# Prompt attention of a hybrid decoder step: values weighed on column halves of the array, sums of probabilities on GpSimd

## The reference, cut to what matters

```python
def fox_prompt(q, k, v, logf):          # q, k, v: (1, 2048, 8, 64)
    ...
        s = jnp.einsum('bqhd,bkhd->bhqk', qi, k).astype(F32) * scale
        s = s + ci.transpose(0, 2, 1)[..., None] - cum_t[:, :, None, :]
        s = jnp.where((qpos[:, None] >= kpos[None, :])[None, None], s, NEG_INF)
        p = jax.nn.softmax(s, axis=-1)
        return jnp.einsum('bhqk,bkhd->bqhd', p.astype(v.dtype), v)
```

## Time and profile before

| | |
|---|---|
| time, median of 3 | 3687.21 us (3680.77 to 3688.68) |
| the profiled execution | 3679.39 us, span 3677.7 us |
| phase of the change | about 1000 to 1978 us of the span |
| TensorE busy, whole span | 3280.4 us (89%) |
| VectorE, ScalarE, GpSimd busy | 1721.9, 1282.1, 296.6 us |

### The profile page before, as it was taken

How to read it: one execution, slowest core, us unless ns; L and a number is a source line. 1 busy time by engine, 2 the same in 40 slices (tenths; PEclk the granted TensorE clock), 3 DMA queues, 4 the chain that set the end, 5 groups by cost and what they waited for, 6 DMA issues and landing times. The chain is left out here.

```text
span 3677.7 us, 63038 instructions
## 1 busy us (share of the span) xinstructions
PE 3280.4 (89%) x22374; PEld 2492.7 (68%) x22374; DVE 1721.9 (47%) x2974; ACT 1282.1 (35%) x2326; POOL 296.6 (8%) x306
## 2 busy tenths in 40 slices
PE   6999789995799899999996859999869999499998
PEld 5888678884465565556554757888747777378887
DVE  3222221242676666667652744333346676443333
ACT  3111121211134334334433533333356666533232
POOL 0000000111211111111100530000000000000000
PEclk9999899996599999999998979999979999699999
DMA  5333442344688888888866863333244433332221
GB/s 140 116 116 115 173 133 96 107 142 124 214 300 285 265 317 281 272 281 312 293 207 204 291 237 121 113 117 127 94 174 138 129 129 109 114 119 91 79 90 59
DMA packets 360931, 627.36 MB, mean 171 GB/s; under 512 B 118185, under 2 KB 180689, under 8 KB 344274
## 3 DMA queue, kind: packets, MB, share of 16 engines
q1 hardware_dynamic: 341410, 487.62, 39.6%
q0 software_dynamic: 19264, 136.46, 10.6%
HBM read 488.74 MB, written 135.22 MB: 170 GB/s over the span
## 5 line engine op out<-in xcount | busy, mean ns | idle before, releaser
L125 PE MATMUL in_ps_z<-in_w_hi,in_u_hi 128*128 128x512 f32 x952 | 375.4, 394 | 41.5 <-DVE in_w_lo L159 41.5
L126 PE MATMUL in_ps_z<-in_w_lo,in_u_hi 128*128 128x512 f32 x952 | 374.3, 393 | 0.0
L127 PE MATMUL in_ps_z<-in_w_hi,in_u_lo 128*128 128x512 f32 x952 | 373.9, 393 | 0.0
L1512 DVE STREAM_TRANSPOSE att_samp_kt<-att_samp_k_ring 128x1024 f32<-128x1024 f32 x256 | 306.9, 1224 | 25.5 <-DMA att_samp_k_ring<-cache_k,att_samp_rows_now 13.2
L1667 PE MATMUL att_fox_ps_o<-att_fox_prob,att_fox_v_one 128*65 128x512 f32 (+3 forms) x640 | 290.4, 537 | 10.1 <-ACT att_fox_prob L1368 9.8
L1368 ACT ACTIVATE att_fox_prob<-att_fox_ps_k 128x512 f32<-128x512 f32 (+1 forms) x320 | 167.6, 531 | 243.6 <-DVE att_fox_ps_k L1480 154.7
L125 PEld LDWEIGHTS in_ps_z<-in_w_hi,in_u_hi 128*128 128x128 f32 x952 | 181.1, 190 | 80.5 <-issue 28.6
L125 PE MATMUL tail_ps_g<-tail_wg_hi,tail_h_hi 128*128 128x512 f32 x544 | 216.3, 398 | 13.6 <-DVE tail_p_lo L2396 9.8
L1461 DVE TENSOR_REDUCE att_fox_part_max<-att_fox_ps_n 128x1 f32<-128x512 f32 (+2 forms) x320 | 193.3, 604 | 75.0 <-PE att_fox_ps_n L1634 65.9
L126 PE MATMUL tail_ps_g<-tail_wg_lo,tail_h_hi 128*128 128x512 f32 x544 | 212.7, 391 | 0.0
L127 PE MATMUL tail_ps_g<-tail_wg_hi,tail_h_lo 128*128 128x512 f32 x544 | 212.6, 391 | 0.0
(11 more groups left out here) (385 smaller groups left out, 6854.6 us busy)
## 6 DMA issues: line engine op xcount, KB each, us to landing
att_samp_v_ring<-cache_v SPq DMA_DIRECT2D x512, 256.0 KB
tail_a_hi<-a_hi SPq DMA_DIRECT2D x34, 512.0 KB, 5.9
tail_a_lo<-a_lo SPq DMA_DIRECT2D x34, 512.0 KB, 6.2
in_w_stage<-w_in_even SPq DMA_DIRECT2D x64, 256.0 KB, 6.6
lru_u_hi<-u_hi SPq DMA_DIRECT2D x8, 2048.0 KB, 8.1
lru_u_lo<-u_lo SPq DMA_DIRECT2D x8, 2048.0 KB, 13.2
in_x<-x SPq DMA_DIRECT2D x17, 512.0 KB, 3.7
u_hi<-in_u_hi SPq DMA_DIRECT2D x17, 512.0 KB, 3.9
```

The source lines that it names most:

```text
L125: pe.matmul(out, act_hi, w_hi, start=start, stop=False)
L126: pe.matmul(out, act_hi, w_lo, start=False, stop=False)
L127: return pe.matmul(out, act_lo, w_hi, start=False, stop=stop)
L1512: ins = dve.transpose(kt[:, n % 2, :, :].rearrange("p c (s i) -> p s c i", s=SLOTS)[:, p * two:(p + 1) * two], k_ring[:, n % KR, p * two * ...
```

## The change

1. `v` loses its column of ones. `weigh` now has 64 stationary columns and writes to partitions 0 to 63 of `ps_o` for even key tiles and 64 to 127 for odd ones.
2. Two weighs follow each other: at odd steps s the list has the weighs of steps s-3 and s-2, at even steps none. In the list their cost is half the sum of their widths; before it was 0.87 each.
3. GpSimd takes the event `exp` (handler `add`): it adds the exponentials of each step to `prob_sum`, 128x512 float32, two buffers. The first two tiles of a group make one addition, so there are 36 per head, and a small copy where the second tile is narrower. `exps` on ScalarE now also waits until the step four before has been added.
4. `turn_out`: the transposes become four matmuls with `o_t` (128 partitions) stationary and a constant `fold` (two 64x64 identities above each other) moving, which turn and add the halves; then, after a wait for the last addition, four matmuls with `prob_sum` stationary and one column of ones moving.
5. GpSimd waits for its newest own work before it starts another. `fold` is loaded with the constants; `ps_o` is zeroed once.

```diff
-                if s >= 2:
+                if s % 2 and s >= 3:
                     g, kt = group_of(s - 2)
-                    out.append((0.87 * cut_width(kt - B4 * g), ("weigh", g, s - 2, kt)))
+                    out.append((0.5 * (cut_width(kt - 1 - B4 * g) + cut_width(kt - B4 * g)), ("weigh", g, s - 3, kt - 1), ("weigh", g, s - 2, kt)))
...
-        v = ph.sb("fox_v_one", [P, 2, PT, HD + 1])
+        v = ph.sb("fox_v", [P, 2, PT, HD])
+        prob_sum = ph.sb("fox_prob_sum", [P, 2, G])
...
-        o_t = ph.sb("fox_o_t", [HD + 1, G])
+        o_t = ph.sb("fox_o_t", [P, G])
...
+            def add(t, i, par, g, s, kt):
+                nonlocal newest
+
+                if kt == 0:
+                    return
+                r, out = max(kt - B4 * g, 0) * P, prob_sum[:, g % 2, :]
+                pool.wait_ge(*exped.at(t, s))
+                if kt == 1:
+                    pool.wait_ge(*(o_turned.at(t, g - 2) if g >= 2 else o_turned.at(t - 1, g - 2 + GQ)))
+                    pool.wait_ge(*newest)
+                    if r:
+                        pool.sem_inc(pool_passed, 1)
+                        pool.tensor_copy(out[:, 0:r], prob[:, (s - 1) % 4, 0:r]).then_inc(first_added.sem, 1)
+                        pool.wait_ge(*first_added.at(t))
+                    ins = pool.tensor_tensor(out[:, r:G], prob[:, (s - 1) % 4, r:G], prob[:, s % 4, r:G], ALU.add)
+                else:
+                    pool.wait_ge(*added.at(t, s - (g + 1) - 1))
+                    pool.wait_ge(*newest)
+                    ins = pool.tensor_tensor(out[:, r:G], out[:, r:G], prob[:, s % 4, r:G], ALU.add)
+                ins.then_inc(added.sem, 1)
+                newest = added.at(t, s - (g + 1))
...
-            one, step = run({"turn": turn, "s_turn": s_turn, "s_exp_new": s_exp_new})
+            one, step = run({"turn": turn, "exp": add, "s_turn": s_turn, "s_exp_new": s_exp_new})
...
                 act.wait_ge(*(weighed.at(t, s - 4) if s >= 4 else weighed.at(t - 1, s - 4 + steps)))
+                act.wait_ge(*added_at(t if s >= 4 else t - 1, s - 4))
...
-                pe.matmul(ps_o[0:HD + 1, r:G], v[:, par, kt, :], prob[:, s % 4, r:G],
-                          start=kt == 0, stop=kt == B4 * (g + 1) - 1).then_inc(weighed.sem, 1)
+                half = slice(kt % 2 * HD, kt % 2 * HD + HD)
+                pe.matmul(ps_o[half, r:G], v[:, par, kt, :], prob[:, s % 4, r:G],
+                          start=kt < 2, stop=kt >= B4 * (g + 1) - 2, skip_group_check=True).then_inc(weighed.sem, 1)
...
                 for b in range(B4):
-                    last = pe.transpose(ps_x[:, b * P:b * P + HD + 1], o_t[:, b * P:(b + 1) * P], ident[0:HD + 1, 0:HD + 1])
+                    halves = HD if g == 0 and b == 0 else P
+                    pe.matmul(ps_x[:, b * P:b * P + HD], o_t[0:halves, b * P:(b + 1) * P], tables.fold[0:halves, 0:HD], start=True, stop=True)
+                pe.wait_ge(*added.at(t, sum(B4 * (x + 1) - 1 for x in range(g + 1)) - 1))
+                for b in range(B4):
+                    last = pe.matmul(ps_x[:, b * P + HD:b * P + HD + 1], prob_sum[:, g % 2, b * P:(b + 1) * P], tables.fold[:, HD:HD + 1],
+                                     start=True, stop=True)
```

More of the change, by code:

```diff
@@ L379, in load @@
     def load(self, sp):
-        for dst, name in [(self.ident, "identity"), (self.mask, "causal_bias"), (self.mask_t, "causal_bias_t")]:
+        for dst, name in [(self.ident, "identity"), (self.mask, "causal_bias"), (self.mask_t, "causal_bias_t"), (self.fold, "fold")]:
             sp.dma_start(dst[:, :], self.io[name]).then_inc(self.consts_in, 16)
@@ L1121, in attention @@
         weighed = ph.count("weighed", steps, 4)
+        added = ph.count("added", steps - GQ)
+        first_added = ph.count("first_added")
         o_copied = ph.count("o_copied", GQ)
@@ L1174, in attention, with added_at @@
         out_kept = ph.count("s_out_kept")
+        def added_at(t, s):
+            s = s if s >= 0 else s + steps
+            g, kt = group_of(s)
+            return added.at(t, s - (g + 1) + (kt == 0))
         def x_free(t, u):
@@ L1288, in _ @@
         def _(pool):
-            lead(pool, doubled, rows_kept)
+            lead(pool, doubled, rows_kept, added, first_added)
+            newest = None
             def gather(b, par, n):
@@ L1317, in turn @@
                 pool.wait_ge(*(doubled.at(t, j - 1) if j else doubled.at(t - 1)))
+                nonlocal newest
+                if newest is not None:
+                    pool.wait_ge(*newest)
+                newest = doubled.at(t, j)
                 pool.sem_inc(pool_passed, 1)
@@ L1328, in s_exp_new @@
                     pool.wait_ge(*k_turned.at(t))
+                    nonlocal newest
+                    pool.wait_ge(*newest)
+                    newest = rows_kept.at(t + 2)
+                    pool.sem_inc(pool_passed, 1)
                     pool.tensor_copy(rows_now[:, par, :], tables.rows[:, bass.ds((t + 2) * NKG, NKG)]).then_inc(rows_kept.sem, 1)
@@ L1339, in _, with head @@
             pool.wait_ge(tables.samp_in, 6 * 16)
-            one, step = run({"turn": turn, "s_turn": s_turn, "s_exp_new": s_exp_new})
+            one, step = run({"turn": turn, "exp": add, "s_turn": s_turn, "s_exp_new": s_exp_new})
             one(-1, -1, 1, opening)
-            each_tile(pool, step, H, peel=2)
+            def head(t, i, par):
+                nonlocal newest
+                pool.wait_ge(*doubled.at(t))
+                newest = added.at(t - 1)
+                step(t, i, par)
+            each_tile(pool, head, H, peel=2)
         @block.scalar
@@ L1372, in copy_out @@
                 act.wait_ge(*(o_turned.at(t, g - 1) if g else o_turned.at(t - 1)))
-                act.copy(o_t[:, :], ps_o[0:HD + 1, :]).then_inc(o_copied.sem, 1)
+                act.copy(o_t[:, :], ps_o[:, :]).then_inc(o_copied.sem, 1)
             def turn(t, i, par, dt, j, u):
@@ L3060, in tables @@
     c["causal_bias_t"] = c["causal_bias"].T
+    c["fold"] = np.concatenate([np.tile(np.eye(HD), (2, 1)), np.ones((P, 1))], axis=1)
     page = page_order(n_pages)
```

13 lines of the change are left out of this document (7 added, 6 removed).

## The result

| | before | after |
|---|---|---|
| time, median | 3684.69 us (3680.77 to 3688.68) | 3745.24 us (3732.32 to 3754.91) |
| profiled execution, span | 3679.39, 3677.7 us | 3732.32, 3730.6 us |
| attention, from 1000 us to its last output | 978.1 us | 1029.8 us |
| granted clock of TensorE, whole span | 0.940 | 0.933 |

Medians are of four executions each, one more of the kernel before than above. The changed kernel is slower: ratio 1.0166, 95% interval 1.0148 to 1.0184, some 61 us. I had forecast 27 us faster, and the time lies above my range too. Of the 52.9 us between the two profiled spans, 51.7 lie in the attention phase. All of the search is therefore in that phase.

The account below looks back on a forecast made before the run. TensorE was taken to bound the phase, VectorE and DMA close behind. Weighs save 110 us, shapes cost 20, group ends 50: 41 at clock 0.97, less 14 of waits, 27 us; forecast 3660 us, range 3612 to 3728.

Parts of the forecast that it names:

- TensorE: 110 - 20 - 50 = 40 us, 41 at clock 0.97: TensorE's attention work: 110 us saved on weighs, 20 added by array shape changes, 50 by group ends.
- Before it waited 12 us; I add 10: TensorE's waits for VectorE's maxima at even steps, 12 us before, would grow by 10 us.
- VectorE takes over: Rival, chance 0.18: TensorE waits 0.2 us more at every second step, 32 us, leaving no measurable gain: 3682.
- Changes of shape: Borders between weighs and matmuls of another array shape: 200 new ones at 0.1 us, 20 us added, bounds 0 and 32.
- Overlap of halves: Paired weighs on two column halves run side by side, a pair costing its wider member: 110 us saved.
- The rival that the halves do not overlap: Paired weighs run one after the other, 70 us slower, 3757; chance 0.09 together with partial overlap, 3710.
- End of a group: Four transposes become eight float32 matmuls, 16 records at 0.11 us: 1.55 us more, 32 times, 50 us added.
- GpSimd: right: Additions of 1.27 us, 305 us in all, leave GpSimd about half busy, not the bound; late gathers cost 4 us.
- GpSimd's order: Rival, chance 0.15: gathers wait behind additions, key slabs land late and TensorE stands; 41 us slower, 3728.
- No slowdown for VectorE: GpSimd's additions beside VectorE's work would not slow VectorE: 0 us; 27 us if every transpose lost a tenth.
- The clock: TensorE's granted clock in the attention phase, taken as 0.97 to turn 40 us of saved work into 41.
- my sign of error, below 0.95: A granted TensorE clock under 0.95 in the attention phase was listed as showing the forecast wrong.

Follow-up runs that it names:

- even list: Changed kernel, list reordered to both scores, look, pair of weighs, look: 3695.49 us, ratio 1.0029; that order on the kernel before, 65 columns: 3669.82 us, ratio 0.9968.
- first experiment: Kernel before, 65 columns, with only the new list of events (weighs paired at odd steps, cost 0.5): 3738.29 us, ratio 1.0151.

## Why the prediction was wrong

*Two steps failed: "TensorE: 110 - 20 - 50 = 40 us, 41 at clock 0.97", and "Before it waited 12 us; I add 10".* I had forecast 41 us less work for TensorE and 14 us more waiting. Between the two profiled phases the busy time rose by 5.6 us and the idle time by 47. So some 47 us of the miss lie in the sum of TensorE's work and some 33 in the waits.

*The waits.* I had named the mechanism in the same paragraph (at even steps nothing stands between two looks) and gave it 10 us for the forecast and 32 for a rival of 0.18. The 12 us were those of the weight loads, 43.1 in the changed kernel; the matmuls themselves went from 2.8 to 25.1. With 65 columns and a cost that fits them the new list costs 32 us by itself. In the changed kernel the even list returns 50; it also gives 12 with 65 columns, so some 38 of the 50 are the repair. What I had not seen is that the look is not alone there. The turns share one bank with VectorE's reads, and two turns also move together (1.0 to 13.4 us of waits), and the sample part waits longer for its reciprocals (3.9 to 11.6) and its values (5.0 to 15.3). I priced one queue, VectorE's maximum, where everything that alternates between TensorE and VectorE had been spaced by the weighs. The rival "VectorE takes over" had the right place and, with 32 us, nearly the price of the list; its time of 3682 came out wrong with the sum that it was taken from.

*The sum of TensorE's work.* Experiments that differ in few things split the 5.6 us (busy time of the phase; the first three lines add up to it by their nature, the split of the second is an estimate):

| step | us |
|---|---|
| the list, 65 columns (first experiment against before) | +12.8 |
| halves without overlap, new end, additions (both weighs on one half against the first experiment; same list) | +96.2 |
| the overlap (changed kernel against both weighs on one half) | -103.4 |
| of the 96.2: end of a group | 53 |
| of the 96.2: clock 0.97 to 0.95 | some 18 |
| of the 96.2: left for changes of shape | some 25 |

Against -110 + 20 + 50 I had too much in the overlap by 7 us and too little in the end by 3 and in the shapes by some 5. The large parts are two terms that I had put at nothing: the clock, and what the list adds to the busy time.

*Changes of shape: a single one too small, the total about right.* I took 0.1 us for each of 200 borders, 20 us, bound 32. A visit costs 0.32 us between ordinary neighbours: I had the 0.14 inside the weigh (1.00 against 0.86) in my rows and counted it as one border, and left out that the matmul ahead of it also loses 0.08. On the average over 160 pairs the 25 us above are 0.16, as many stand beside a quarter block, where part was paid before. That the two errors nearly cancel is luck. The Trainium skill, "TensorEngine Tiling (Array Packing)", section "Tiling Modes", has the drain at a change of mode; the trace agrees that the change costs time, 0.32 us in the visit above, and the price is the row's.

*Overlap of halves: right.* Four records in 1.00 us, and 103 us more busy time when both weighs go to one half. The rival that the halves do not overlap is out, although the two weighs are issued one after the other.

*End of a group: right.* 50 us forecast. The eight fold records take 1325.09 - 1324.15 = 0.94 us and the sums' about as much: 1.9 against the 0.21 of before, 32 times 53 us; the busy time into `ps_x` rose by 51.5.

*GpSimd: right.* Additions at 1.28 us mean for full width, no gain without them and 1 to 10 us of cost when they are added alone. The key slabs bear it. Idle time ahead of the gathers by releaser, and who waited for them, changed kernel:

```profile
  ACT att_fox_prob L1416: 55.1, 23
...
  DVE att_samp_kt L1560: 12.7, 13
```

The first row is idle time that ended with the exponentials, for which only the additions wait, 55.1 us ahead of 23 gathers; the second is VectorE waiting for slabs, 12.7 us in 13 places, against 13.2 in 11 before. The rival "GpSimd's order" would have shown here.

*No slowdown for VectorE: wrong, without a price.* I argued from the large transposes, which kept their time. The tiny products did not: the product with -1 had a median of 169 ns before (L1471) and 824 after (L1519), up to 1955. It cost no time that the runs could tell. The Trainium skill, "SBUF — State Buffer", section "SBUF: two separate sides", says that VectorE and GpSimd share a port pair under an exclusive lock. The delays here, 0.65 us at the median and at most 1.79 beside additions of 1.27, agree with it in kind; the longest are more than one addition, and that it is this lock is not shown.

*The clock: put at 0.97 on both sides without a reason.* Over the same 960 us of the phase:

```profile
1000.00:1960.00 960.00, 898.45 (x10560) 561.95 (x10563) 619.44 (x1124) 377.20 (x872) 143.07 (x178) 0.97 0.83 277
...
1000.00:1960.00 960.00, 859.53 (x10512) 546.66 (x10512) 633.91 (x1094) 357.93 (x826) 428.01 (x444) 0.94 0.82 270
```

That is 0.97 before and 0.94 after (0.95 with the last 70 us), so my sign of error, below 0.95, did show. On 915 us of busy time 2 to 3 points are some 18 to 27 us, an estimate.

*What the change is worth.* Compared list by list, the halves with additions and a float32 end are no gain anywhere: 5 us slower on the uneven list with costs of 0.5 (within noise), 29 on the uneven list when the 65 columns have their own cost, 23 on the even list. An overlap worth 82 us pays for the end of a group, the shapes and the clock, and no more. So the list explains 32 to 38 of the 61 us (56 by the first experiment, whose costs fit the halves and not the 65 columns), and the rest would be there without it.

**What stays open.** All nine kernels with 64-column halves had a lower granted clock over the whole span of the profiled execution, 0.925 to 0.934, and all five with 65 columns 0.940 to 0.944, whatever their list or their additions. The one with both weighs on one half is among the low ones, so it is not the overlap. Three things always came together: the 64 columns, the change of shape, and the new end of a group with its 8 or 16 small matmuls. No run separates them. The traces speak for a share of the end: in the phase before, the clock fell to its lower level (1.2 of 2.4 GHz) 7 times, 51 us in all, 2 of them within 4 us behind the end of a group; in the changed kernel 16 times, 113 us, 8 of them within 4 us behind it. But the other falls also went from 5 to 8, and with the additions alone, where the end is the old one, 6 of 7 lay near an end. One of those of the changed kernel: the fold and sum matmuls run from 1455.55 to 1457.49, TensorE then idles 0.88 us until VectorE has read `ps_x`, and the granted clock is 1.00 from 1455 to 1459 us and 0.57 from 1459 to 1463.

Nor is it shown which part of the even list does the work, the weighs between the looks or the scores moved together. And the split of the idle time in the changed kernel among maxima, turns and sample work is not exact: the waits are of one execution each, and they shift one another.

## What to carry to other kernels

When pieces of work are put side by side so that they can overlap, look at what they were standing between. Here the weighs spaced everything that went back and forth between TensorE and VectorE, and the list that kept them between the looks was worth 32 to 38 us, nearly half of the 82 that the overlap gives. Try a new order on the old kernel too: here it gained 12 us by itself, which would otherwise have been counted for the halves. Price a change of array shape at all three places: the matmul ahead, the block itself, the matmul behind. Price small float32 matmuls by their records: 16 records with 1 to 64 moving columns are 1.9 us, and one record each in fp32r halves it. Do not carry the granted clock over from the kernel before; read it again.

## What the runs showed of the hardware

- Two float32 matmuls of 512 columns and two records each take 1.00 us on two column halves; one alone on a half takes 1.00 too (the last timeline above), one with 65 stationary columns 0.86.
- A 128x4 instruction of VectorE beside GpSimd's additions took up to 1955 ns instead of 170, and when it was replaced by one that was not delayed (157 ns), the next took the delay (median 164 to 612 ns). Without the additions it took 170 to 173 ns.
- The granted clock was 0.92 to 0.95 in the phase of the kernels with halves and their end of a group, and 0.97 to 0.98 in that of the kernels without.
